# Five modulation units ahead of the S5 kernel rows, and two jobs handed to other engines, in a four-stage encoder trunk

## The chip, the cores and the metric

The kernel runs on one core of one Trainium2 chip. The core has five engines that run side by side and meet only at semaphores: TensorE (PE in the profile; PEld is its weight loading), VectorE (DVE), ScalarE (ACT), GpSimd (POOL) and SyncE (SP), which here only issues DMAs. The metric is the device time of one execution in microseconds (us); lower is better. Times inside an execution are counted from the start of the span that the profiler saw.

## The reference

One sequence of 512 tokens with 1024 features goes through an S5 layer and a differential-attention layer, each followed by a gated MLP with a causal convolution. Around each of the four stands a sandwich of norms and a modulation that comes from one conditioning vector:

```
for i in range(DEPTH):                       # DEPTH = 2
    mod = cond @ ada_w[i] + ada_b[i]         # 1024 x 6144, for one vector
    sh_t, sc_t, g_t, sh_c, sc_c, g_c = jnp.split(mod, 6, axis=-1)
    h = modulate(rms_norm(x, norm_g[i, 0]), sh_t, sc_t)
    h = s5_mixer(h, ...) if i % 2 == 0 else diff_attention(h, ...)
    x = x + g_t[:, None, :] * rms_norm(h, norm_g[i, 1])
    h = modulate(rms_norm(x, norm_g[i, 2]), sh_c, sc_c)
    h = conv_ffn(h, ffn_w_in[i], ffn_conv_w[i], ffn_conv_b[i], ffn_w_out[i])
    x = x + g_c[:, None, :] * rms_norm(h, norm_g[i, 3])
```

All is float32. The S5 mixer is a complex diagonal recurrence over the tokens for 64 groups of 16 channels, followed by a gelu and a gated product (GLU).

## The kernel before

**Precision and weights.** A large product is made of three matmuls: each operand is split into a rounded high part and the rest, its low part. Weights come in units of 128 x 2048 (1 MB) into two buffers `raw`. ScalarE copies a unit to `whi` (`split_high`, L803), and VectorE makes `wlo = raw - whi` (`split_low`, L1426; GpSimd does it for the first two units, L597). The semaphore `split_lo` counts the units whose low part is there.

**The first stage, S5.** In the first 126 us nothing is a plain product of that kind. In order of time:
- VectorE and GpSimd compute powers, input matrices and output matrices of the recurrence (`cl_re`, `cl_im`, `rot_c`, `rot_s`).
- TensorE turns the input matrices in four groups of four banks, `turned_inputs(0)` to `(3)` (L1952), and ScalarE copies each bank (`copy_inputs`, L747).
- Between them TensorE multiplies the conditioning vector with the 24 *modulation units* of layer 0, 1 MB each (`ada_unit`, L1913; unit n is `ada_raw` in the slot `ADA0_SLOT[n]`). Units 0 to 7 give the shift, 8 to 15 the second third of the row and 16 to 23 the last. All 24 add up in one PSUM bank, so the first unit of a third waits until ScalarE has copied the third before it out (`copy_row`, L727).
- The modulation of the first input is spread by one small matmul (L1977), and ScalarE applies it to the input u in 16 quarters (`scaled`, L759). The semaphore `u_ready` counts the four pieces of u.
- `inputs(piece)` (L1991) gives the driving term of the recurrence, which VectorE then scans (L1454 to L1482). `kernel_rows` (L2050) makes the 16 x 16 x 8 blocks of the short convolution, and after its last matmul ScalarE copies them (`kx`, L790), GpSimd adds the skip term (L583), and SyncE spreads them by 32 DMAs, eight to a piece, into four block-Toeplitz buffers `toep` that were cleared before (`load_toeplitz`, L333).
- `local(piece)` (L2009) multiplies u with a Toeplitz buffer, `carried(piece)` (L2027) adds what the state carries in, and `back(piece)` (L2038) turns the gelu of the sum, which is the operand of the GLU products (from L2129 on).

**Order.** Every engine runs a list written out by hand. SyncE's queue is one list as well: 24 modulation units, then the Toeplitz loads with the first two weight units between them. A load of a modulation unit waits until the unit that was in its slot before is used (`ada_used`). Slots 0 and 1 are the two `raw` buffers, slots 2 and 3 are the first two Toeplitz buffers, and slots 4 to 6 lie where the input matrices of `turned_inputs(2)` and `(3)` stood, so they are free only after these (`inb_psum`).

**Between the first MLP and attention** stands `barrier(1)`: sums of squares, two roots by GpSimd (L605), and then `next_input(1)` on VectorE, which per feature tile f gates the branch (`gate_late`, L1578), adds it to x (tiles 0 and 1 on VectorE, L1507, 2 to 7 on GpSimd, L608), scales it (`scale`, L1599) and makes the low part (`low`, L1586). TensorE follows tile by tile with the products for the attention values. After tile 3 VectorE also makes the low part of the value weights' second unit:

```
next_input(1, {3: lambda: split_low(U_V + 1, 1, None)})
```

Of the kernel before, what the change touches and what calls it, by code (L numbers as in the profile page):

```python
# [17 lines left out]
F32 = mybir.dt.float32  # L18
F32R = mybir.dt.float32r
I32 = mybir.dt.int32  # L20
ALU = mybir.AluOpType
# [3 lines left out]
P = 128  # L25
D = 1024
SEQ = 512
KT = D // P
# [11 lines left out]
OCTS = 4  # L40
# [21 lines left out]
ADA0_SLOT = 4 * (0, 1, 2, 3) + (6, 4, 5, 0, 1, 6, 4, 5)  # L62
# [14 lines left out]
def build(nc, a, out_rows):  # L77

    ctx = ExitStack()
    with ctx:  # L80
# [320 lines left out]
        def _(sp):  # L401
# [17 lines left out]
            for piece in range(OCTS):  # L419
                load_toeplitz(sp, piece)  # L420
                if piece % 2:
                    n = piece // 2
                    sp.wait_ge(ada_used, 20 + n)
                    sp.dma_start(raw[:, n, :], a["units"][n]).then_inc(raw_landed[n], 16)
# [60 lines left out]
        def _(pool):  # L485
# [73 lines left out]
            def decay_tile(piece):  # L559

                wait(pool, scanned, piece - 1)
                dst, g = decays[piece % 2], slice(PO * piece, PO * piece + PO)
                link(nc.gpsimd.tensor_copy(dst, s5s[:, 18, g].unsqueeze(2).broadcast_to([P, PO, NB])))
                nc.gpsimd.memset(dst[:, :, 0], 0.0).then_inc(decay_ready, 1)
# [7 lines left out]
            decay_tile(1)  # L572
# [6 lines left out]
            pool.wait_ge(ada_used, 2 * KT)  # L579
            for i in range(2):  # L580
                nc.gpsimd.memset(toep[i][:], 0.0).then_inc(toep_clear, 1)
            pool.wait_ge(k_copied, 4)
            nc.gpsimd.tensor_tensor(kx[:, 0], kx[:, 0], tk, ALU.add).then_inc(k_ready, 1)  # L583
            pool.wait_ge(hx_im, 2)
# [15 lines left out]
            def residual(r):  # L600

                pool.wait_ge(const_ready, 5)
                for root, ready, n in ((stat[:, 16:16 + QT], r1_ready, 1), (stat[:, 20:20 + QT], r2_ready, 2)):
                    pool.wait_ge(root_arg, 2 * r + n)
                    nc.gpsimd.tensor_tensor(root, nwt[:, 0, 0:QT], power[:], ALU.pow).then_inc(ready, 1)  # L605
                for f in POOL_X[r]:
                    pool.wait_ge(gated, KT * r + f + 1)
                    nc.gpsimd.tensor_tensor(x[:, f, :], x[:, f, :], y_of(r)[:, f, :], ALU.add).then_inc(x_pool, 1)  # L608
# [69 lines left out]
        def _(act):  # L678
# [101 lines left out]
            copy_inputs(3, partial(scaled, 0))  # L780
            for quarter in range(3):
                scaled(1, quarter)
            copy_row(1)
            store_row(1, 0)
            scaled(1, 3)
            for quarter in range(2):
                scaled(2, quarter)
# [5 lines left out]
            for quarter in range(2, 4):  # L793
                scaled(2, quarter)
            for quarter in range(4):
                scaled(3, quarter)
# [364 lines left out]
        def _(dve):  # L1161
# [574 lines left out]
            next_input(1, {3: lambda: split_low(U_V + 1, 1, None)})  # L1736
# [6 lines left out]

            split_low(U_V + 2, 0, None)
# [158 lines left out]
        def _(pe):  # L1903
# [54 lines left out]
            def ada_units(lo, hi):  # L1958

                for n in range(lo, hi):  # L1960
                    ada_unit(n)
# [13 lines left out]
            turned_inputs(2, (2, 3))  # L1975
            pe.wait_ge(umod_rhs, 2)
            M(psum[:, 7, P:P + 2 * GROUPS], sel16[:].rearrange("p t c -> p (t c)"),  # L1977
              ca[:, 0, 0:2 * GROUPS], start=True, stop=True).then_inc(umod_psum, 1)
            turned_inputs(3)
            ada_units(13, 14)  # L1980
# [77 lines left out]
            ada_units(14, 15)  # L2058
# [4 lines left out]
            ada_units(15, 16)  # L2063
            kernel_rows(range(2, 4))
            ada_units(16, 17)
            kernel_rows(range(4, 6))
            ada_units(17, 18)
            kernel_rows(range(6, PO)).then_inc(k_psum, 1)
            inputs(1)
            ada_units(18, 20)  # L2070
            carried(0, True)
            ada_units(20, 22)
            inputs(2)
            ada_units(22, N_ADA_PE)
            local(0, False)
            carried(1, True)
            inputs(3)
            local(1, False)
# [571 lines left out]
```

## Time and profile before

| | |
|---|---|
| Median of 3 runs | 1212.21 us (1211.85 to 1215.84) |
| The profiled execution: its own time, its span | 1210.92 us, 1209.1 us |
| PE busy | 1171.6 us, 97% of the span |
| DVE, ACT, POOL busy | 61%, 43%, 33% |
| The chain that ended last | PE 83%, DVE 9%, issue 2%, SP queue 2%, ACT 2% |
| Busy in 100 to 110 us | PE 9.88, DVE 8.13, ACT 7.01, POOL 1.49 of 10 us |

The profile comes from one execution. TensorE is busy nearly all the time, so what counts is where it is idle or slow, and that is the first 126 us and the barriers. The chain that ended last is followed back from the last instruction, at each step to what released it; a part of it on another engine than TensorE is a place where the kernel waited for that engine. [...]

### The profile page before, as it was taken

The page shows a single profiled execution, that of the slowest core. Times are in us where ns is not written, and L with a number is a line of the kernel's source. Part 1 is how long each engine was busy: PE and PEld are TensorE (multiplying, and loading weights), DVE is VectorE, ACT ScalarE, POOL GpSimd, SP SyncE. Part 2 cuts the span into 40 slices and gives each one's busy share as a digit, 9 for nine tenths or more (in the row PEclk, how much of TensorE's full clock was granted, in tenths as well). Part 3 has the DMA queues.
Part 4 walks back from the last instruction along what each step waited for, and adds up shares of the span by engine and source line. Part 5 has one row for each costly group of instructions (what it writes and reads, how often), then busy time and mean ns, then how long its engine had stood idle before and what let it go on. Part 6 is the DMA issues. An engine that isn't in the chain of part 4 may idle for free.

```text
span 1209.1 us, 17510 instructions
## 1 busy us (share of the span) xinstructions
PE 1171.6 (97%) x6508; PEld 934.6 (77%) x6508; DVE 737.0 (61%) x974; ACT 520.0 (43%) x792; POOL 393.8 (33%) x272
## 2 busy tenths in 40 slices
PE   5789999999999999999999999999999999999998
PEld 2458888788787888888787777677788888888887
DVE  8998687979863553243854777948644444442323
ACT  4466444443443342143423677755434443442311
POOL 4973100366553431000305345402343334420000
PEclk9999999999999999999999999999999999999999
DMA  9887655177633323231223322211222222223221
GB/s 374 339 271 179 260 204 207 45 268 255 249 122 105 104 75 135 103 106 70 83 105 105 105 78 80 88 35 70 105 105 76 97 104 104 91 97 125 92 82 70
DMA packets 34984, 162.25 MB, mean 134 GB/s; under 512 B 12768, under 2 KB 13088, under 8 KB 16688
## 3 DMA queue, kind: packets, MB, share of 16 engines
q1 hardware_dynamic: 25632, 161.15, 37.5%
q10 hardware_dynamic: 9296, 0.34, 0.6%
q8 instruction: 37, 0.61, 0.2%
q14 instruction: 19, 0.16, 0.0%
HBM read 152.79 MB, written 2.13 MB: 128 GB/s over the span
## 4 chain that ended last, share of the span: by engine, by line
PE 83%; DVE 9%; issue 2%; SPq 2%; ACT 2%; POOL 1%; DMA 1%; DVEq 0%; POOLq 0%; ACTq 0%
PE psum L2095 17%; PE psum L2097 17%; PE psum L2096 17%; PE psum L2361 3%; PE psum L2360 3%; PE psum L2362 3%; PE psum L2263 3%; PE psum L2264 3%; PE psum L2265 3%; SPq L333 2%; PE psum L2421 1%; PE psum L2442 1%; PE psum L2409 1%; PE psum L2129 1%; PE psum L2403 1%
## 5 line engine op out<-in xcount | busy, mean ns | idle before, releaser
L2095 PE MATMUL psum<-hhi,whi 128*128 128x512 f32 x896 | 352.0, 393 | 0.9 <-DVE wlo L1426 0.9
L2097 PE MATMUL psum<-hhi,wlo 128*128 128x512 f32 x896 | 348.9, 389 | 0.0
L2096 PE MATMUL psum<-hlo,whi 128*128 128x512 f32 x896 | 348.8, 389 | 0.0
L1426 DVE TENSOR_TENSOR wlo<-raw,whi 128x2048 fp32r<-128x2048 f32 x79 | 187.9, 2378 | 185.0 <-ACT whi L803 185.0
L803 ACT ACTIVATE whi<-raw 128x2048 fp32r<-128x2048 f32 x80 | 153.2, 1914 | 166.9 <-PE psum L2362 74.3
L615 POOL TENSOR_TENSOR ca<-ca,cb 128x512 f32<-128x512 f32 x44 | 137.6, 3126 | 235.7 <-ACT ca L963 235.7
L2095 PEld LDWEIGHTS psum<-hhi,whi 128*128 128x128 f32 x896 | 168.5, 188 | 38.5 <-issue 2.1
L2097 PEld LDWEIGHTS psum<-hhi,wlo 128*128 128x128 f32 x896 | 168.2, 188 | 35.1
L2096 PEld LDWEIGHTS psum<-hlo,whi 128*128 128x128 f32 x896 | 168.3, 188 | 34.1
L1626 DVE SCALAR_TENSOR_TENSOR ca<-psum,convp,ca 128x511 f32<-128x511 f32 x44 | 32.9, 749 | 182.6 <-ACT ca L958 182.6
L965 ACT ACTIVATE ghi<-ca 128x512 f32 (+1 forms) x44 | 27.8, 633 | 149.4 <-POOL ca L615 149.4
L958 ACT ACTIVATE ca<-psum,convp 128x512 f32<-128x512 f32 x44 | 34.2, 778 | 114.2 <-PE psum L2097 106.7
L617 POOL TENSOR_TENSOR glo<-ca,ghi 128x512 f32 (+1 forms) x44 | 67.8, 1542 | 40.3 <-ACT ghi L965 40.3
L605 POOL TENSOR_TENSOR stat<-nwt,power 128x4 f32<-128x4 f32 x6 | 6.4, 1069 | 220.2 <-DVE nwt L1555 216.3
L2263 PE MATMUL psum<-whi,ghi 128*128 128x512 f32 x176 | 68.7, 391 | 0.0
L2265 PE MATMUL psum<-whi,glo 128*128 128x512 f32 x176 | 68.5, 389 | 0.0
L2264 PE MATMUL psum<-wlo,ghi 128*128 128x512 f32 x176 | 68.5, 389 | 0.0
L2360 PE MATMUL psum<-ghi,whi 128*128 128x512 f32 x176 | 68.5, 389 | 0.0
L2361 PE MATMUL psum<-glo,whi 128*128 128x512 f32 x176 | 68.5, 389 | 0.0
L2362 PE MATMUL psum<-ghi,wlo 128*128 128x512 f32 x176 | 68.5, 389 | 0.0
L1493 DVE SCALAR_TENSOR_TENSOR ada_acc<-ada_ring,cond,ada_acc 128x2048 f32<-128x2048 f32 x24 | 62.4, 2602 | 0.0
L1055 ACT ACTIVATE prob<-psum,stat 128x128 f32<-128x128 f32 (+3 forms) x64 | 33.1, 523 | 17.7 <-DVE stat L1772 17.3
(411 smaller groups left out, 1846.5 us busy)
## 6 DMA issues: line engine op xcount, KB each, us to landing
raw<-in_units SPq DMA_DIRECT2D x92, 1024.0 KB, 4.8
ada_raw<-in_ada_w SPq DMA_DIRECT2D x24, 1024.0 KB, 8.2
ada_ring<-in_ada_w SPq DMA_DIRECT2D x24, 1024.0 KB, 4.8
qk_sw<-ca SPq DMA_DIRECT2D x32, 128.0 KB, 2.3
u<-in_x_blocks SPq DMA_DIRECT2D x1, 2048.0 KB, 9.7
x<-in_x_t SPq DMA_DIRECT2D x1, 2048.0 KB, 8.2
out_rows<-y_late SPq DMA_DIRECT2D x8, 256.0 KB, 2.0
bc_par<-in_s_bc SPq DMA_DIRECT2D x1, 1024.0 KB, 4.9
```

Source lines behind the costliest of these rows:

```text
L615: nc.gpsimd.tensor_tensor(ca[:, s, :], ca[:, s, :], cb[:, s, :], ALU.mult).then_inc(g_ready, 1)
L803: A(whi[:, s, :], raw[:, s, :], ACT.Copy).then_inc(split_hi, 1)
L1426: TT(wlo[:, s, :], raw[:, s, :], whi[:, s, :].bitcast(F32), ALU.subtract).then_inc(split_lo, 1)
L2095: M(out, w_hi, hi[:, k, :], start=(k == 0), stop=False)
L2096: M(out, w_hi, lo[:, k, :], start=False, stop=False)
L2097: return M(out, w_lo, hi[:, k, :], start=False, stop=(k == KT - 1))
L2263: M(out, ghi[:, row, tok], whi[:, s, w], start=(isinstance(v, int) and row == 0), stop=False)
L2264: M(out, ghi[:, row, tok], wlo[:, s, w], start=False, stop=False)
L2265: return M(out, glo[:, row, tok], whi[:, s, w], start=False, stop=(isinstance(v, int) and row == JT - 1))
L2360: M(out, whi[:, s, w], ghi[:, row, :], start=(fixed and row == 0), stop=False)
L2361: M(out, whi[:, s, w], glo[:, row, :], start=False, stop=False)
L2362: return M(out, wlo[:, s, w], ghi[:, row, :], start=False, stop=(fixed and row == JT - 1))
```

## The change

Five things change:
- **TensorE's order.** Units 13 to 17 now come before `inputs(0)`; before, units 14 to 17 stood after it. Two units stay between the kernel rows (18 and 19, where three stood), and units 20 to 23 follow `inputs(1)` in one piece. `local(1)` moves ahead of `inputs(3)`.
- **Slots.** Units 17 to 23 get other slots, so that units 17 and 18 need no slot of the input matrices.
- **ScalarE.** The copy of the second third of the modulation row (`copy_row(1)`) moves between the scaling of quarters 2 and 3 of the first piece, its store right after that, and all of piece 1 is scaled ahead of the wait for the kernel rows. ScalarE clears the first Toeplitz buffer (128 x 2048), with a copy of a zero column.
- **GpSimd** clears only the second Toeplitz buffer, and does it after it has added the skip term.
- **The value weights' second unit.** Its low part is made by GpSimd in `barrier(1)`, after the two roots and ahead of the six additions to x; VectorE no longer makes it.

```
-ADA0_SLOT = 4 * (0, 1, 2, 3) + (6, 4, 5, 0, 1, 6, 4, 5)
+ADA0_SLOT = 4 * (0, 1, 2, 3) + (6, 0, 1, 4, 5, 0, 1, 6)
...
             decay_tile(0)
-            decay_tile(1)
...
-            pool.wait_ge(ada_used, 2 * KT)
-            for i in range(2):
-                nc.gpsimd.memset(toep[i][:], 0.0).then_inc(toep_clear, 1)
             pool.wait_ge(k_copied, 4)
             nc.gpsimd.tensor_tensor(kx[:, 0], kx[:, 0], tk, ALU.add).then_inc(k_ready, 1)
+            decay_tile(1)
+            pool.wait_ge(toep_clear, 1)
+            pool.wait_ge(ada_used, 2 * KT)
+            nc.gpsimd.memset(toep[1][:], 0.0).then_inc(toep_clear, 1)
...
+                if r == 1:
+                    pool.wait_ge(split_hi, U_V + 2)
+                    nc.gpsimd.tensor_tensor(wlo[:, 1, :], raw[:, 1, :], whi[:, 1, :].bitcast(F32),
+                                            ALU.subtract).then_inc(split_lo, 1)
...
-            copy_inputs(3, partial(scaled, 0))
-            for quarter in range(3):
+            def scaled_first(quarter):
+
+                scaled(0, quarter)
+                if quarter == 2:
+                    copy_row(1)
+
+            copy_inputs(3, scaled_first)
+            store_row(1, 0)
+            for quarter in range(4):
                 scaled(1, quarter)
-            copy_row(1)
-            store_row(1, 0)
-            scaled(1, 3)
-            for quarter in range(2):
-                scaled(2, quarter)
+            act.wait_ge(const_ready, 5)
+            act.wait_ge(ada_used, 2 * KT)
+            A(toep[0][:].rearrange("p k q c -> p (k q c)"), ac_w[:, W_A, 1:2].broadcast_to([P, UNIT]),
+              ACT.Copy).then_inc(toep_clear, 1)
             act.wait_ge(k_psum, 1)
...
-            next_input(1, {3: lambda: split_low(U_V + 1, 1, None)})
+            next_input(1, {})
...
+            dve.wait_ge(split_lo, U_V + 2)
             split_low(U_V + 2, 0, None)
...
             turned_inputs(2, (2, 3))
+            ada_units(13, 15)
             pe.wait_ge(umod_rhs, 2)
...
-            turned_inputs(3)
-            ada_units(13, 14)
+            turned_inputs(3, (0, 1))
+            ada_units(15, 16)
+            turned_inputs(3, (2, 3))
+            ada_units(16, 18)
...
             inputs(0)
-            ada_units(14, 15)
...
             kernel_rows(range(0, 2))
-            ada_units(15, 16)
-            kernel_rows(range(2, 4))
-            ada_units(16, 17)
-            kernel_rows(range(4, 6))
-            ada_units(17, 18)
-            kernel_rows(range(6, PO)).then_inc(k_psum, 1)
+            ada_units(18, 19)
+            kernel_rows(range(2, 5))
+            ada_units(19, 20)
+            kernel_rows(range(5, PO)).then_inc(k_psum, 1)
             inputs(1)
-            ada_units(18, 20)
+            ada_units(20, N_ADA_PE)
             carried(0, True)
-            ada_units(20, 22)
             inputs(2)
-            ada_units(22, N_ADA_PE)
             local(0, False)
             carried(1, True)
+            local(1, False)
             inputs(3)
-            local(1, False)
             back(0)
```

TensorE's list from `turned_inputs(2, (2, 3))` to the first kernel rows, before (L1952 `turned_inputs`, L1977 the small matmul of the modulation, L1913 a modulation unit, L1991 `inputs`, L2050 the kernel rows; `ada_raw_79` to `_85` are slots 0 to 6):

```order
L1952 MATMUL psum<-ident,lb_69 128x128 x16
L1977 MATMUL psum<-ca,sel_96 128x128
L1952 MATMUL psum<-ident,lb_70 128x128 x32
L1913 MATMUL psum<-ada_raw_80,cond 1x512 x4
L1991 MATMUL psum<-u,inb_re 64x64 x16
L1991 MATMUL psum<-u,inb_im 64x64 x16
L1913 MATMUL psum<-ada_raw_81,cond 1x512 x4
L2050 MATMUL psum<-cl_re,kb 16x128 x8
```

The same stretch of the changed kernel (its line numbers are 10 to 13 higher):

```order
L1962 MATMUL psum<-ident,lb_69 128x128 x16
L1923 MATMUL psum<-ada_raw_80,cond 1x512 x4
L1923 MATMUL psum<-ada_raw_81,cond 1x512 x4
L1988 MATMUL psum<-ca,sel_96 128x128
L1962 MATMUL psum<-ident,lb_70 128x128 x16
L1923 MATMUL psum<-ada_raw_82,cond 1x512 x4
L1962 MATMUL psum<-ident,lb_70 128x128 x16
L1923 MATMUL psum<-ada_raw_85,cond 1x512 x4
L1923 MATMUL psum<-ada_raw_79,cond 1x512 x4
L2004 MATMUL psum<-u,inb_re 64x64 x16
L2004 MATMUL psum<-u,inb_im 64x64 x16
L2063 MATMUL psum<-cl_re,kb 16x128 x8
```

Units 13 and 14 now stand ahead of the small matmul, unit 15 inside `turned_inputs(3)`, and 16 and 17 between it and `inputs(0)`; behind `inputs(0)` the kernel rows follow at once.

GpSimd's list around the skip term, the lines that go (-) and come (+); `toep_75` and `toep_76` are the first two Toeplitz buffers:

```order
 L563 COPY decay<-s5s 128x512
 L564 MEMSET decay 128x8
+L576 TENSOR_TENSOR cb<-sel_96,dskip 128x256
+L579 TENSOR_TENSOR kx<-kx,cb 128x256
 L563 COPY cb<-s5s 128x512
 L564 MEMSET cb 128x8
-L577 TENSOR_TENSOR cb<-sel_96,dskip 128x256
-L581 MEMSET toep_75 128x2048
-L581 MEMSET toep_76 128x2048
-L583 TENSOR_TENSOR kx<-kx,cb 128x256
+L583 MEMSET toep_76 128x2048
```

The addition to `kx` has moved ahead of the second decay tile and of the one clearing that is left here.

GpSimd's list of the changed kernel in `barrier(1)`, from the two roots on:

```order
L605 TENSOR_TENSOR stat<-nwt,power 128x4 x2
L608 TENSOR_TENSOR wlo<-raw,whi 128x2048
L612 TENSOR_TENSOR x<-x,y_late 128x512 x6
L635 TENSOR_TENSOR gdiag<-ident,gate 128x1024
L645 TENSOR_TENSOR qk<-ca,cosb 128x512 x2
```

The row L608 is new: before, the six additions followed the roots directly.

## Rows read from the trace of the kernel before

**Rows 1.** Chain of waits, 53 to 111 us: start, us, what.

```profile
53.10 1.63 PE psum L1952 x8
...
65.16 1.75 PE psum L1913 x8
...
67.98 0.97 PE psum L1913 x8
...
75.00 2.07 ACT kx L790 x4
...
78.43 0.60 SPq L333
...
103.33 4.37 DMA toep<-kx
...
110.74 3.66 PE psum L2027 x128
```

**Rows 2.** Timeline of PE: start, us, what, xcount [idle before <-releaser].

```profile
52.62 0.49 PE L1977 MATMUL psum<-ca,sel 128*128 128x128 f32 x2 [2.51 <-DVE ca L1399]
...
62.30 1.16 PE L1991 MATMUL psum<-u,inb_re 128*64 128x64 f32 x32 [2.97 <-ACT u L759]
...
74.87 1.15 PE L1991 MATMUL psum<-u,inb_re 128*64 128x64 f32 x32
...
76.88 1.90 PE L1913 MATMUL psum<-ada_raw,cond 128*1 128x512 f32 x16
...
106.53 1.10 PE L2038 MATMUL psum<-ident,z 128*128 128x128 f32 x8
```

**Rows 3.** Windows: length, busy PE PEld DVE ACT POOL, PEclk, DMA, GB/s.

```profile
54.00:55.00 1.00, 1.00 (x7) 1.00 (x6) 0.96 (x3) 0.19 (x1) 0.84 (x3) 0.50 0.89 369
...
64.00:65.00 1.00, 1.00 (x22) 0.97 (x19) 0.69 (x3) 1.00 (x4) 0.85 (x1) 0.50 1.03 434
```

**Rows 4.** Timeline of ACT, 60 to 106 us.

```profile
60.72 5.41 ACT L759 ACTIVATE u<-u,s5s 128x64 f32<-128x64 f32 x16
69.01 0.60 ACT L727 ACTIVATE sq<-psum 128x512 f32<-128x512 f32 x1 [2.88 <-PE psum L1913]
69.64 1.05 ACTq L732 DMA_DIRECT2D mod_rows<-sq  x1
...
103.99 1.93 ACT L803 ACTIVATE whi<-raw 128x2048 fp32r<-128x2048 f32 x1
```

**Rows 5.** DMA view, issued 42.40 to 42.67 us (unit 14): KB, us to landing.

```profile
ada_raw<-in_ada_w SPq DMA_DIRECT2D x1, 1024.0 KB, 9.6
```

**Rows 6.** DMA view, issued 60.00 to 60.40 us (unit 20).

```profile
ada_raw<-in_ada_w SPq DMA_DIRECT2D x1, 1024.0 KB, 12.1
```

**Rows 7.** Timeline of DVE, the scans of the recurrence.

```profile
81.59 1.39 DVE L1460 TENSOR_TENSOR v_re<-v_re,ca 128x512 f32<-128x512 f32 x1
...
107.69 0.69 DVE L1482 SCALAR_TENSOR_TENSOR rot_c<-v_re,rot_s 128x504 f32<-128x504 f32 x1
```

**Rows 8.** Timelines of POOL, DVE and PE in barrier(1), and POOL at 108 us.

```profile
581.09 1.01 POOL L605 TENSOR_TENSOR stat<-nwt,power 128x4 f32<-128x4 f32 x1 [1.34 <-DVE nwt L1573]
586.17 2.55 POOL L608 TENSOR_TENSOR x<-x,y_late 128x512 f32<-128x512 f32 x2 [4.06 <-DVE y_late L1578]
...
584.02 0.69 DVE L1507 TENSOR_TENSOR x<-x,y_late 128x512 f32<-128x512 f32 x1
...
588.76 0.74 DVE L1586 SCALAR_TENSOR_TENSOR hlo<-psum,modt,hhi 128x512 fp32r<-128x512 f32 x1
...
591.53 2.94 DVE L1426 TENSOR_TENSOR wlo<-raw,whi 128x2048 fp32r<-128x2048 f32 x1
...
589.65 1.10 PE L2409 MATMUL psum<-whi,hlo 128*128 128x512 f32 x4
...
596.44 1.20 PE L2409 MATMUL psum<-whi,hlo 128*128 128x512 f32 x4 [1.15 <-DVE hlo L1586]
...
108.51 4.62 POOL L597 TENSOR_TENSOR wlo<-raw,whi 128x2048 fp32r<-128x2048 f32 x1 [14.05 <-DVE rot_c L1482]
```

More of the change, by code:

```diff
@@ L422, in _ @@
                     n = piece // 2
-                    sp.wait_ge(ada_used, 20 + n)
+                    sp.wait_ge(ada_used, 22 + n)
                     sp.dma_start(raw[:, n, :], a["units"][n]).then_inc(raw_landed[n], 16)
@@ L792, in _ @@
                   ACT.Copy).then_inc(k_copied, 1)
[L793 to L796, printed above, removed]
+            for piece in range(2, OCTS):
+                for quarter in range(4):
+                    scaled(piece, quarter)
             def split_high(n, s, half):
```

## The prediction

> **What bounds the kernel now.** I read the busy times first: TensorE works 97% of the span, so a change pays only where TensorE is idle or slow and everything behind it hangs on that place. Then the chain of waits, in order of time, for the stage that the diff touches. It runs over the last group of turned matrices and ScalarE's scaling to `inputs(0)` at 62.30, over a modulation unit (65.16) to the kernel rows, and at 75.00 it leaves TensorE for ScalarE's copy of them [rows 1, 2]. GpSimd's addition follows, and from 78.43 on the chain is SyncE's queue: 32 Toeplitz loads one after another until the last one, issued at 103.33, lands at 103.33 + 4.37 = 107.70 [rows 1]. Only then can `local(3)` run, then `back(2)` and `carried(3)`, which ends at 110.74 + 3.66 = 114.40 [rows 1], and the GLU products start.
>
> [...] First, TensorE's own list is as long as the queue: its last work ahead of `local(3)`, a `back`, ends at 106.53 + 1.10 = 107.63 [rows 2], 0.07 us before the load lands. So both must get shorter together. [...]
>
> VectorE is the third list. It computes without a pause and ends its part of the stage at 107.69 + 0.69 = 108.38 [rows 7]; the last quarter of `carried(3)`, which needs that result, begins about 0.9 us before 114.40, so there are 5 us of room.
>
> The other place is `barrier(1)`. VectorE's `wlo` (2.94 us from 591.53) holds back the low part of tile 3, and TensorE idles 1.15 us for it at 596.44 [rows 8].
>
> **The kernel rows, part by part.**
>
> *Unit 14 ahead of the small matmul.* Its load is issued at about 42.5 and takes 9.6 us [rows 5], so it is there at 52.1. One unit takes 0.97 us [rows 1] and the small matmul starts at 53.1 where it started at 52.62 [rows 2]: 0.5 late. Unit 13 fills the gap before that and costs nothing.
>
> *The first eight transposes behind it.* They took 1.63 us at half clock [rows 1]; eight of the same shape take 1.10 at full clock (the `back`) [rows 2]. With two units in the 2.51 us gap I expect the full clock: 0.5 early.
>
> *ScalarE's copy of the modulation row* is now inside the chain: 0.60 [rows 4], of which 0.1 overlaps its neighbour: 0.5 late. The three together put `inputs(0)` at 62.30 + 0.5 - 0.5 + 0.5 = 62.8.
>
> *Units 15, 16 and 17.* TensorE has to wait in `turned_inputs(3)` for ScalarE's copies anyway, so unit 15 is free. Unit 16 begins a new third and waits for `copy_row(1)`, which ScalarE reaches about 2.4 us before its last scaling ends: one copy and one quarter (5.41 / 4 = 1.35 us [rows 4]) stand behind it. Units 16 and 17 need 2 x 0.97 = 1.94 us, so they end just before 62.8. They are hidden by the same scaling that TensorE idled for; without that cover they would cost 1.94.
>
> *`inputs(0)` and unit 14.* At half clock they took 65.16 - 62.30 = 2.86 and 1.76 (to 66.92, as 65.16 + 1.75 says) [rows 1, 2]. At full clock `inputs` takes 76.88 - 74.87 = 2.01 [rows 2], and unit 14 is gone. I take the full clock: 62.8 + 2.01 = 64.8.
>
> *The kernel rows.* From 66.92 to 75.00 there are 8.08 us with three units; two units stay, so 8.08 - 0.97 = 7.11. They end at 64.8 + 7.1 = 71.9 instead of 75.0. **That is 3.1 us.** Of it, 1.76 + 0.97 are two units that left the stretch, 0.85 is the clock, and 0.5 is given back in front.
>
> *What could hold ScalarE up.* After the first piece, at 62.7, it issues the store (1.05), scales piece 1 (16 instructions, 5.41) and clears a Toeplitz buffer, an operation that no row shows. Its nearest row is the copy of a 128 x 2048 unit, 1.93 [rows 4]; a bound below is nothing, one above is GpSimd's 4.62 for that size [rows 8]. With 1.93 ScalarE is at the kernel rows at 62.7 + 1.1 + 5.4 + 1.9 = 71.1, 0.8 us ahead of 71.9. At 4.62 it would be 1.9 us late, and the gain 1.2.
>
> *The loads.* SyncE is past its last modulation unit before the rows end, and the loads of 17 and 18 go out at 50 to 51 us, in a stretch where the queue waited for a slot. GpSimd reaches `kx` early, for it clears nothing before. So the first Toeplitz load goes out at 78.43 - 3.1 = 75.3, and the last lands at 104.6. Everything that GpSimd does later (second decay tile, second clearing) is needed 6 us after that at the earliest.
>
> *TensorE's list from there.* It has 2 units fewer behind the rows (6 before, 4 now: 1.9 us) and starts 3.1 us earlier, but `carried(1)` and `carried(2)` wait for VectorE, whose times stay. Counting the list through with the full-clock durations it is at `local(3)` at 104 to 105, level with the load at 104.6. `local(1)` ahead of `inputs(3)` swaps two waits that are both over by then. So the GLU products start 3.1 us earlier. If the Toeplitz loads got through faster, because units 22 and 23 no longer share the DMA engines with them, VectorE's waits would cap it at about 3.7.
>
> **`barrier(1)`.** The wait of 1.15 goes. GpSimd's second root ends at 581.09 + 1.01 = 582.10; its `wlo` takes 4.62 [rows 8] and ends at 586.7. The addition for tile 2 began at 586.17, so it is 0.55 late. VectorE's scaling of tile 2 and the low part of tile 1 queue behind it. That low part ended at 588.76 + 0.74 = 589.50 and TensorE took it at 589.65 [rows 8], so 0.4 of it reach TensorE. VectorE's own addition at 584.02 has two SBUF operands and runs beside the new instruction; such an instruction took 1.39 instead of 0.69 beside GpSimd [rows 7, 8], so up to 0.7. The two overlap in the same queue: I take 0.65, between 0.4 and 1.1. Net 1.15 - 0.65 = **0.5 us**, between 0 and 0.75.
>
> **Sum.** 3.1 + 0.5 = 3.6 us from the profiled execution's own 1210.9, so 1207.3. The median of the runs lies 1.3 above that execution, and I predict on it: 1212.2 - 3.6 = 1208.6.
>
> **The rivals.**
>
> *A, the clock falls all the same.* TensorE is through `turned_inputs(3)` at about 58.2 and idles until `copy_row(1)` is done at 60.4: a gap of 2.2 us, hardly shorter than the two that were followed by half clock [rows 2, 3]. For it: those two. Against it: it has units on both sides. If units 16, 17 and `inputs(0)` run at half clock, that costs what it cost before, about 0.85 + 0.8 = 1.7 us: 1210.3. [...]
>
> *B, VectorE or the DMA engines become the bound.* GpSimd's additions fall on other VectorE instructions than before. Three prolonged as in [rows 7], by 0.7 each, would delay VectorE by 2.1 and `carried(1)` and `carried(2)` with it: the gain falls to about 1.5, 1210.7. For it: VectorE has no idle time there to make it up. Against it: GpSimd has less to do than before in that stretch.
>
> *C, slower: a load is late.* Unit 17 is now needed at 61.6, about 11 us after its load can be issued; before, it had 14. All of `inputs(0)` stands behind it. At 12.1 us, the longest of this stretch [rows 6], it comes at 62.7 and costs 1.1. It decides from 14.6 us on, when the 3.6 are used up; at 19 us the time would be 1216.6. Against it: only unit 16's load and older ones stand ahead of it.
>
> *D, VectorE is shut out in `barrier(1)`.* If its addition at 584.02 has to wait until GpSimd's `wlo` ends at 586.7, it is 2.65 late, and so is TensorE: 1.15 - 2.65 = -1.5, with the 3.1 a gain of 1.6: 1210.6. Against it: an instruction of that kind was 0.70 longer beside GpSimd, not shut out [rows 7]. [...]
>
> *E, more.* The full cap (3.7) and a barrier with little loss (0.75 to 1.15): 1207.5.
>
> **How the numbers follow.** Forecast 0.44 (1207.9 to 1209.4, since each term moves by some tenths), A 0.22, B 0.12, C 0.06, D 0.05, E 0.11. A range of 1207.1 to 1211.0 leaves out C, a part of E and the far ends of A, B and D, about 0.2. About 0.3% (3.6 us) is what a measurement of this kernel can tell from no change, and the forecast lies on that bound. Faster by more: half of the forecast's cases (0.22), all of E, and 0.07 of A and B where their price is half of the one above: 0.40. Within: 0.54. Slower: 0.06.
>
> **What would show it.** Right: the copy of `kx` starts near 71.9, the first Toeplitz load near 75.3, the last lands near 104.6, `carried(3)` ends near 111.3; the clock is 1.00 from 53 to 67; TensorE has no idle ahead of L1977 but 1 us before unit 14, and one of about 2 us before unit 16; in `barrier(1)` the idle ahead of the low step of tile 3 is gone and 0.6 stands ahead of that of tile 0 or 1. Wrong: a clock of 0.50 anywhere between 59 and 67 (A); VectorE's last scan after 109 (B); TensorE's idle time ahead of unit 14, 17 or 18 put down to a DMA (C); ScalarE's clearing above 2.7 us; or a stall behind 126 us that takes back what the first stage gave.

## The result

The change makes the kernel slower, by half a per cent.

| | before | after |
|---|---|---|
| Median of 9 runs each, same chip | 1211.85 us (1209.68 to 1215.84) | 1218.49 us (1216.14 to 1221.55) |
| Ratio, 95% interval | | 1.0052 [1.0041, 1.0063] |
| The profiled execution: own time, span | 1210.92, 1209.1 us | 1219.39, 1217.6 us |

Forecast was 1208.6 (1207.1 to 1211.0), with 0.06 for slower: wrong in sign. The medians differ by 6.6 us and the two profiled executions by 8.5: that of before lies 0.9 below its median, that of after 0.9 above its own. The 8.5 us between the two spans can be followed by anchors: the first GLU product starts 4.5 later (118.83 instead of 114.32), `barrier(1)` adds 2.9, and the attention stage some 1.0, where TensorE waits 3.0 us in all for `att` (L1797) instead of 2.0. That last 1.0 I did not follow further.

**Up to the kernel rows the profile after is what the forecast drew.** Timeline of PE, columns as in [rows 2]:

```profile
52.23 1.04 PE L1923 MATMUL psum<-ada_raw,cond 128*1 128x512 f32 x8 [1.04 <-DMA ada_raw<-in_ada_w]
...
60.81 1.90 PE L1923 MATMUL psum<-ada_raw,cond 128*1 128x512 f32 x16 [2.52 <-ACT sq L731]
62.64 1.15 PE L2004 MATMUL psum<-u,inb_re 128*64 128x64 f32 x32
```

Units 16 and 17 hide in the wait for ScalarE, `inputs(0)` starts at 62.64 (62.8 forecast) and the first row at 64.66 (64.8). Then comes what no step of the forecast had:

```profile
69.28 0.31 PE L2063 MATMUL psum<-cl_re,kb 64*16 64x128 f32 x5 [1.76 <-issue]
...
76.85 0.39 PE L2063 MATMUL psum<-cl_im,kb 64*16 64x128 f32 x1 [4.49 <-issue]
...
78.24 1.97 PE L2004 MATMUL psum<-u,inb_re 128*64 128x64 f32 x32
...
81.85 4.18 PE L1923 MATMUL psum<-ada_raw,cond 128*1 128x512 f32 x32
```

In the middle of the rows TensorE stands still twice, for 1.76 and 4.49 us, and the profile names no releaser: "issue" is time in which it waited for nothing that the profile shows. `inputs(1)` behind it takes 3.61 us (78.24 to 81.85) instead of the 2.01 of [rows 2]. ScalarE then waits for TensorE (timeline of ACT):

```profile
67.68 1.91 ACT L796 ACTIVATE toep<-ac_w 128x2048 f32<-128x2048 f32 x1
78.35 2.06 ACT L800 ACTIVATE kx<-psum 128x512 f32<-128x512 f32 x4 [8.76 <-PE psum L2063]
```

ScalarE's clearing took 1.91 (1.93 forecast), and then it idled 8.76 us for the rows. Windows of the stretch show the clock (PEclk, the granted share of full speed; 0.50, which in before stands behind the idle times of 2.51 and 2.97 us [rows 2, 3], is "half clock" below) and the DMA engines (columns as in [rows 3]), first after, then before:

```profile
70.00:73.00 3.00, 2.37 (x94) 1.01 (x79) 2.96 (x5) 0.00 (x0) 2.52 (x4) 1.00 0.96 391
73.00:75.00 2.00, 0.00 (x0) 0.00 (x0) 1.97 (x3) 0.00 (x0) 0.00 (x0) 1.00 0.46 188
75.00:77.00 2.00, 0.15 (x8) 0.15 (x16) 1.90 (x4) 0.00 (x0) 0.00 (x0) 0.80 0.05 12
77.00:80.00 3.00, 3.00 (x66) 2.48 (x56) 1.08 (x2) 1.65 (x4) 0.00 (x0) 0.50 0.02 5
```

```profile
70.00:73.00 3.00, 2.40 (x77) 1.15 (x81) 2.96 (x5) 2.26 (x7) 2.81 (x7) 1.00 0.15 33
```

After has the DMA engines full until 73.5 us; before had them nearly idle (0.15) in 70 to 73. VectorE runs out of work in 77 to 80 as well (busy 1.08 of 3 us). And the DMA view has, beside the kernel's own queue, one called "instruction", with packets of 16 KB (37 packets, 0.61 MB on the page of after and on that of before). These are the windows 74.6 to 74.7 us of after and 71.8 to 71.9 us of before (queue, kind: packets, MB, share):

```profile
q8 instruction: 1, 0.02, 58.2%
```

```profile
q8 instruction: 1, 0.02, 59.9%
```

Before has a packet at 71.83 and after none until 74.63, 1.1 us after the engines drained, and TensorE resumes 2.2 us behind it.

**In `barrier(1)`**, timelines of POOL, DVE and PE after, answering to [rows 8]:

```profile
586.62 4.81 POOL L608 TENSOR_TENSOR wlo<-raw,whi 128x2048 fp32r<-128x2048 f32 x1
...
588.56 3.42 DVE L1516 TENSOR_TENSOR x<-x,y_late 128x512 f32<-128x512 f32 x1
...
594.08 1.28 PE L2417 MATMUL psum<-whi,hlo 128*128 128x512 f32 x4 [2.48 <-DVE hlo L1595]
595.15 0.63 PE L2411 MATMUL psum<-whi,hhi 128*128 128x512 f32 x1
```

VectorE's addition takes 3.42 us instead of 0.69. It ends at 591.98, 0.55 us after GpSimd's subtraction (586.62 + 4.81 = 591.43). TensorE idles 2.48 for it, and its next matmuls start 0.43 apart instead of 0.23: half clock (0.50 from 596 to 598). Against the first product of the stage (589.52, before 584.98) the low step of tile 5 stands 2.9 us later than before (609.44, before 602.01).

### The profile page after: what moved, and what is told of

Same layout as the page of the kernel before. It is cut to its first block, busy times and chain, and to the rows that moved or that the text cites. A ratio compares the mean times of both kernels' runs of the same rounds, so it can differ in the third digit from the quotient of the medians.

```text
span 1217.6 us, 17514 instructions
## 1 busy us (share of the span) xinstructions
PE 1173.3 (96%) x6508; PEld 935.7 (77%) x6508; DVE 739.1 (61%) x973; ACT 521.5 (43%) x793; POOL 397.2 (33%) x272
## 4 chain that ended last, share of the span: by engine, by line
PE 85%; DVE 5%; DMA 3%; issue 2%; SPq 2%; ACT 1%; POOL 1%; DVEq 0%; POOLq 0%; ACTq 0%
PE psum L2103 17%; PE psum L2105 17%; PE psum L2104 17%; PE psum L2368 3%; PE psum L2370 3%; PE psum L2369 3%; PE psum L2273 3%; PE psum L2271 3%; PE psum L2272 3%; SPq L333 2%; PE psum L2429 1%; DMA ada_raw<-in_ada_w 1%; PE psum L2417 1%; PE psum L2411 1%; PE psum L2412 1%
```

## The experiments

Two theories stood against each other for the rows. **F**: TensorE's instructions come through the same DMA engines, and their packet waits behind the modulation loads in the queues. **L**: the new order itself, five rows on end without a unit, uses instructions up faster than they come. For the barrier: **P**, VectorE's addition is shut out while GpSimd works, against **Q**, something else. "Rows" below is the start of ScalarE's copy of `kx`, "GLU" the first product of L2129; before has 75.00 and 114.32. A ratio is to the kernel before, run on the same chip beside the experiment, with its 95% interval in brackets. Experiments 4 to 7 were timed once: they are read by their traces, not by their times.

**1. The barrier's part alone.** To the kernel before, only this is added, with its wait on VectorE:

```
+                if r == 1:
+                    pool.wait_ge(split_hi, U_V + 2)
+                    nc.gpsimd.tensor_tensor(wlo[:, 1, :], raw[:, 1, :], whi[:, 1, :].bitcast(F32),
+                                            ALU.subtract).then_inc(split_lo, 1)
-            next_input(1, {3: lambda: split_low(U_V + 1, 1, None)})
+            next_input(1, {})
+            dve.wait_ge(split_lo, U_V + 2)
```

> The kernel before, with one part of the change: the low part of the value weights' second unit made by GpSimd. The rest is as before. Theory P (VectorE's addition of tile 1 is shut out for as long as GpSimd's instruction runs, TensorE idles 2.5 us for it and falls to the half clock): the addition takes about 3.4 us instead of 0.69, TensorE idles about 2.5 us ahead of the first low step and runs the next 3 us at half clock, the time rises by 3 to 4.5 us. Rival Q (what the profile of the changed kernel shows in the barrier is a consequence of the disturbed first stage, and by itself the step is worth the 0.5 us of the prediction): 0 to 1 us faster.

Ratio 1.0019 [1.0008, 1.0030], span 1210.3. Timelines of DVE and PE:

```profile
583.31 3.42 DVE L1511 TENSOR_TENSOR x<-x,y_late 128x512 f32<-128x512 f32 x1
```

```profile
588.83 1.20 PE L2414 MATMUL psum<-whi,hlo 128*128 128x512 f32 x4 [2.48 <-DVE hlo L1590]
```

The same 3.42 and 2.48, so P. The clock stayed at 1.00 behind it in this execution, and the stage cost 1.3 us, not 2.9: the 1.6 between them is the half clock that the execution of after had behind the same gap (eight matmuls 0.43 apart instead of 0.23). The 3 to 4.5 us that I had expected for the whole were too many: the ratio makes 2.3.

**2. The first stage's part alone:** the changed kernel with `barrier(1)` as before.

```
-                if r == 1:
-                    pool.wait_ge(split_hi, U_V + 2)
-                    nc.gpsimd.tensor_tensor(wlo[:, 1, :], raw[:, 1, :], whi[:, 1, :].bitcast(F32),
-                                            ALU.subtract).then_inc(split_lo, 1)
-            next_input(1, {})
+            next_input(1, {3: lambda: split_low(U_V + 1, 1, None)})
-            dve.wait_ge(split_lo, U_V + 2)
```

> The changed kernel with the value weights as before, so the first stage's part of the change alone. Both theories of the first stage expect two idle stretches of TensorE inside the kernel rows, about 1.8 and 4.5 us, put down to nothing that the profile shows, and 2 to 4.5 us more than the kernel before. Rival Q expects most of the change's 6.6 us here, 6 us or more.

Ratio 1.0021 [1.0009, 1.0032], span 1213.6. Issue stalls of 1.15 and 2.84 us in the rows, rows 78.17, GLU 118.14. The stalls are shorter than in after, in the same places. Each part costs some 2.4 us by itself; the product of the two ratios, 1.0040, is near the whole's 1.0052 and leaves 1.4 us that lie within the intervals.

**3. Units 22 and 23 loaded late.** As 2, but their loads wait for the end of the rows:

```
+                if n == N_ADA_PE - 2:
+                    sp.wait_ge(k_psum, 1)
                 sp.dma_start(ada0_raw[slot][:], ...)
```

> As e2_s5_only, but SyncE waits until the kernel rows are done before it issues the loads of modulation units 22 and 23. Theory F (TensorE's next instructions are fetched by the same DMA engines and come behind the modulation loads that are queued there): the DMA engines run dry near 70 us, the long idle stretch of 4.5 us in the kernel rows shrinks to under 1 us, the rows end at 72 to 74 instead of 78, and units 22 and 23 are waited for instead, 1 to 3 us; the time is 2 to 5 us below e2_s5_only, and at or below the kernel before. Theory L (the list itself is the cause: with fewer long matmuls between the small ones TensorE uses up its instructions faster than they can come, whatever the DMA engines do): the idle stretches stay, and the time is that of e2_s5_only or above it, for the late loads cost extra.

Ratio 1.0005 [0.9993, 1.0017]. Stalls 1.82 and 0.65, rows 75.42, GLU 116.30. TensorE's list is that of 2, and of the long stall 0.65 is left: F. The late units are waited for, 1.49 and 2.05 us, a little more than the 1 to 3 that I had expected, and the copy starts at 75.42, not at 72 to 74, for the first stall stayed. The intervals of 2 and 3 overlap, so it is the trace that shows the gain, not the time.

**4. Units 21 to 23 loaded in part.** As 2, with 128 of 2048 columns of these units loaded, so that part of layer 0's modulation comes from old data:

```
+                c = slice(0, UNIT if n < N_ADA_PE - 3 else P)
+                sp.dma_start(ada0_raw[slot][:, c], a["ada_w"][n][:, c])...
```

> As e2_s5_only, but the loads of modulation units 21 to 23 bring the first 128 of 2048 columns only, so part of the modulation of layer 0 is made of old data; everything else is computed. Theory F: the DMA engines are idle from about 68 us, the long idle stretch in the kernel rows goes (under 0.7 us), and the rows end near 72 to 73. Theory L: it stays at 4 us or more, since TensorE's list is the same.

1213.01 us (one run), stalls 1.84 and 0.37, rows 74.28. Same list, no long stall, no late unit. The first stall stayed, and with it the rows are later than the 72 to 73 that I had expected.

**5. Also units 17 and 18 in part.** As 4, with `n in (17, 18, 21, 22, 23)` cut.

> This is the changed kernel with barrier(1) as in the kernel before, and the loads of units 17, 18 and 21 to 23 bring only the first 128 of 2048 columns (part of layer 0's modulation is then made from old data); units 16, 19 and 20 are loaded whole. TensorE's list is unchanged. The question is the first of the two stalls in the kernel rows, the one near 70 us that the profile puts down to issue (1.15 us in the run with units 21 to 23 whole, 1.84 with them small). Theory F (TensorE's instructions are fetched through the same DMA engines, and the fetch waits behind the modulation loads in the queue): with some 2 MB less in the queue between 58 and 70 us the packet of instructions that starts at 67.6 to 68.5 in the runs so far starts 1.5 to 5 us earlier, and the first stall shrinks below 0.5 us; no second stall; the rows end at 72.0 to 72.8, kx at 72 to 73. Rival L (the rows' small matmuls use up the instructions faster than any fetch brings them): the stall stays at 1.1 to 1.9 us wherever the packet starts.

1209.49 us (one run), span 1207.7. The packets of instructions come at 65.46 and 69.46, and timeline of PE:

```profile
71.86 0.28 PE L2059 MATMUL psum<-cl_im,kb 64*16 64x128 f32 x1 [0.50 <-issue]
```

Both stalls together are 0.50, rows 72.73, GLU 111.70. A second profile of this kernel (14) has 0.59. So the first stall too was the queue's.

**6. The kernel before with more traffic.** TensorE's list untouched; two copies of 1 MB from DRAM to DRAM ahead of the load of unit 21, which nothing reads:

```
+                if n == N_ADA_PE - 3:
+                    for i in range(2):
+                        sp.dma_start(spare[i], a["units"][i]).then_inc(par_in, 16)
```

> This is the kernel before, TensorE's list unchanged, with two copies of 1 MB from DRAM to DRAM that nothing reads, which SyncE issues behind the load of unit 20 (about 60 us), so that the DMA engines stay busy from 69.75 to 73.25 us, where they were idle in the kernel before (share 0.08 and less) and where its packet of instructions at 71.83 came. Theory F: that packet comes when the copies have drained, at 74 to 76 us, and the kernel rows get a stall of 2 to 4 us put down to issue that the kernel before does not have (its only one there is 0.61 us); the rows end at 77 to 79 instead of 74.9, and the span grows by 2 to 4 us. Rival L (the stall comes from TensorE's own order, five rows in a row without a unit): no stall over 1 us in the rows, since the order is that of before, and the rows end by 75.5; the loads of units 21 to 23 may land up to 5 us later in either case, which the waits for them would show as DMA.

1217.53 us (one run), span 1215.7. Timeline of PE, and windows:

```profile
77.76 0.37 PE L2054 MATMUL psum<-cl_re,kb 64*16 64x128 f32 x1 [3.02 <-issue]
```

```profile
70.00:72.00 2.00, 1.45 (x32) 0.38 (x33) 1.97 (x4) 1.16 (x4) 1.88 (x5) 1.00 0.96 414
...
78.00:80.00 2.00, 2.00 (x42) 1.52 (x28) 0.40 (x1) 1.20 (x3) 0.00 (x0) 0.50 0.95 389
```

The packet of 71.83 comes at 75.33, and the order of before gets the stall and the half clock of after. This is the reverse of 3 to 5: traffic alone makes the stall, whatever the order. L falls. No unit was waited for. The span grew by 6.6 us where I had expected 2 to 4; the copy of the rows starts 3.8 later than in before and the GLU 5.8 (120.08).

**7. GpSimd's `wlo` behind VectorE's additions.** As 1, with a wait ahead of it:

```
+                    pool.wait_ge(x_dve, 2 * KT - len(POOL_X[0]) - len(POOL_X[1]))
```

> This is the kernel before with GpSimd making the low part of the value weights' second unit, as in the first experiment, but only after VectorE's second addition to x (GpSimd waits for it). Theory P (the two exclude each other: an addition with both operands in SBUF stands still while GpSimd works): VectorE's addition takes 0.69 us again instead of 3.42, GpSimd's low part runs from 584.7 to 589.5 us and the additions of tiles 2 to 7, now GpSimd's next work, start at 589.5 instead of 586.2; TensorE waits 1.5 to 2.5 us for the high or low part of tile 2 and hardly after that. Rival Q' (the 3.42 us came from a slow access to these addresses, whatever GpSimd does): the addition still takes 3 us or more.

1220.34 us (one run). Timelines of DVE and PE:

```profile
588.31 0.69 DVE L1512 TENSOR_TENSOR x<-x,y_late 128x512 f32<-128x512 f32 x1
```

```profile
597.02 2.07 PE L2415 MATMUL psum<-whi,hlo 128*128 128x512 f32 x4 [2.92 <-DVE hlo L1591]
```

The addition takes 0.69 again, beside an idle GpSimd: P holds, Q' falls. My 1.5 to 2.5 us for TensorE was low: it waits 2.92, and with the half clock behind it (0.50 from 597 to 601) the stage is 4.5 us longer than before. 4.3 of the span's growth lay ahead of the barrier, with the first stage as before but an issue stall of 2.02 and a Toeplitz wait of 3.32 us: one execution of the old order differs from another by so much.

**8. Units 22 and 23 behind `inputs(2)`**, and else as 3:

```
-            ada_units(20, N_ADA_PE)
+            ada_units(20, 22)
             carried(0, True)
             inputs(2)
+            ada_units(22, N_ADA_PE)
```

> This is the changed kernel with barrier(1) as before, the load of unit 22 (and 23 behind it) held until the kernel rows are done, and, new in this run, units 22 and 23 moved behind inputs(2), where the kernel before had its last two. Theory F: the long stall stays gone as in the run with the late loads (0.65 us left there), and the two waits for the late loads (1.49 and 2.05 us there, with a stretch at half clock behind them) shrink below 0.5 us together, since the units come some 6 us later; the first stall of 1 to 2 us stays. Carried(0) ends near 82; the ratio to the kernel before is 0.997 to 1.000. Rival M (the waits move on to the next late thing, the Toeplitz pieces, which the loads of units 22 and 23 at 76 to 81 us delay): the waits for Toeplitz data before local(1) to local(3) add up to over 2 us and the ratio stays at 1.000 to 1.001.

Ratio 1.0005 [0.9984, 1.0027]. The waits for units are gone, as expected, but a new issue stall of 1.95 stands in `inputs(2)` at 84.76, where the Toeplitz loads, which stand behind the held loads in the queue, fill the engines (DMA share 1.13 in 82 to 84 us), and `local(3)` waits 2.25 for its piece. GLU 116.28, as in 3. This is rival M.

**9. The low part one tile later**, in the kernel before: `next_input(1, {4: ...})`.

> This is the kernel before with one number changed: VectorE makes the low part of the value weights' second unit after tile 4 of next_input(1) instead of after tile 3. Theory W (the wait of 1.15 us at 596.4 is only the low part of tile 4 behind 2.94 us of VectorE, and one tile later TensorE is further behind): the wait before the low-part matmuls of tile 4 goes, VectorE starts the weight's low part near 594, and at most 0.5 us is given back at tile 5; 0.5 to 1.2 us gained, a ratio of 0.9990 to 0.9997. Rival (the lead is no larger one tile on, since VectorE needs 2.12 us per tile and TensorE 2.75): a wait of 0.9 to 1.5 us at tile 5 takes its place, and the ratio is 1.000 within 0.0005.

Ratio 0.9999 [0.9985, 1.0012]. The wait of 1.15 is gone and 0.40 stands at the next tile; from the first product to the low step of tile 5 the stage is 0.6 us shorter. That is W's size in the trace, and the interval neither shows it nor rules it out.

**10, 11 and 12. The loads held back further.** 10 is the kernel before with `if n == 19: sp.wait_ge(k_psum, 1)`; 11 adds the edit of 9; 12 is 8 with `n == 20` and the edit of 9.

> This is the kernel before, TensorE's list unchanged, with the load of unit 19 (and those of 20 to 23 behind it) held until the kernel rows are done. Theory F (instructions are fetched behind the queued loads): only three loads (16 to 18) are in the queue from 58 us, the DMA engines are free from about 67 to 74.5 us, the packets of instructions near 68 and 72 us find them idle and start 0.5 to 2 us earlier, and the stall put down to issue in the rows (0.61 us in one execution of before, 1.06 and 2.02 us in two others with the same order) is below 0.5 us. The five loads then come from 74.5 to 87 us: unit 19 is waited for up to 0.7 us at 77.8 us, and the Toeplitz pieces, 32 DMAs behind them, may land up to 2 us later. Net a ratio of 0.9985 to 1.0005. Theory L (the rows outrun any fetch): the stall keeps its 0.6 to 2.0 us and the late loads only add, a ratio of 1.0005 to 1.003.

> This is the kernel before with both edits: the loads from unit 19 on held until the kernel rows are done, and the low part of the value weights' second unit after tile 4. The two places are 500 us apart, so the gains should add: a ratio of 0.9980 to 1.0000 if theories F and W hold, 0.9995 to 1.0030 if neither does.

> This is the changed kernel with barrier(1) as before but the low part after tile 4, units 22 and 23 behind inputs(2), and the loads from unit 20 on held until the kernel rows are done. Four loads (16 to 19) are in the queue from 58 us and drain by 67.5 us. Theory F: the stall put down to issue near 70 us (1.52 us with five loads in the queue) falls to 0.5 us or less, the rows end at 72.5 to 73.5 us, unit 20 is waited for 0 to 1.5 us, and VectorE, which works without a pause from 68.9 us on, is the next limit, as the reading of before had it as a rival. Ratio 0.9980 to 0.9995. Rival M (the loads held back come into the way of the Toeplitz pieces and of the packets of instructions near 82 us, where the run before this had a stall of 1.95 us): the gain in the rows is given back by 112 us, ratio 0.9995 to 1.0010.

| | ratio | issue stalls in the rows | rows | waits for units | GLU |
|---|---|---|---|---|---|
| 10 | 1.0053 [1.0034, 1.0072] | none | 72.76 | 2.08, 2.50 | 119.17 |
| 11 | 1.0048 [1.0033, 1.0063] | none | 74.71 | 4.44, 0.33 | 122.79 |
| 12 | 1.0011 [0.9996, 1.0027] | none | 72.93 | 2.88, 1.41 | 116.75 |

In all three the stall in the rows is gone, with either order, which is F once more. And in all three the time is lost again, against the ratios that I had expected (0.9985 to 1.0005, 0.9980 to 1.0000 and 0.9980 to 0.9995): the first held unit (19, in 12 unit 20) comes 2.1 to 4.4 us late, not the 0.7 that I had, since its load started only at the end of the rows and took 4.9, 7.3 and 4.8 us to land in 10, 11 and 12. Holding loads back made no room here; in 10 it costs as much as the whole change.

**13 and 14. Both orders without the load pressure.** Five units loaded in part in each, with the modulation partly from old data: 13 is the kernel before with units 19 to 23 cut, 14 is the kernel of 5, timed.

> This is the kernel before, TensorE's list unchanged, in which the loads of units 19 to 23 bring only the first 128 of 2048 columns (part of layer 0's modulation is then made from old data): the control of the next run. With the DMA engines free from about 67 us on, theory F expects no stall over 0.5 us put down to issue in the rows, kx at 74.0 to 74.9, and, the Toeplitz pieces being alone in the queue, the first GLU product at 112.5 to 114; a ratio of 0.997 to 0.9995 to the kernel before. If the forecast's 3.1 us of order were real, this run must be slower than the next one.

> This is the changed kernel with barrier(1) as before, in which the loads of units 17, 18 and 21 to 23 bring only their first 128 columns, as in a run before, now timed beside its control. In both runs five loads are cut and the DMA engines are free from about 67 us, so the difference between the two is TensorE's order (and ScalarE's and GpSimd's part) without the loads. Theory O (the forecast's reading of the order was right: the rows end 3.1 us earlier once nothing holds the instructions up, and what follows keeps it): kx at 72 to 73, the first GLU product 1.5 to 3 us before that of the control, and a ratio lower by 0.0012 to 0.0025 than the control's. Rival B (VectorE and the Toeplitz pieces are the bound behind the rows): kx is earlier by 2 us or more, but the first GLU product by less than 0.8 us, and the ratios agree within 0.0007.

| | ratio | stall in the rows | rows | GLU | span |
|---|---|---|---|---|---|
| 13, old order | 0.9995 [0.9981, 1.0010] | 0.28 | 73.81 | 113.73 | 1210.1 |
| 14, new order | 0.9986 [0.9975, 0.9997] | 0.59 | 72.73 | 110.95 | 1207.0 |

In these two profiles the new order starts the rows' copy 1.1 us and the GLU 2.8 us earlier; by the medians it is 1213.11 against 1211.55, 1.6 us, and the intervals overlap. The ratio is lower by 0.0009, less than Theory O asked for and more than rival B did. A gain of the order, where the loads are taken away, is likely by this and not shown: there is one profile of the control, and the old order by itself has its GLU anywhere between 113.62 and 118.64. With all loads in place no version with the new order is faster than the kernel before (after, 2, 3, 8 and 12 have ratios of 1.0005 to 1.0052).

## Why the prediction was wrong

- **Unit 14, the transposes, `copy_row(1)`: right.** `inputs(0)` at 62.64 instead of 62.8.
- **Units 15 to 17 hidden, full clock in `inputs(0)`: right in this execution (2.02 us), by luck.** Of the eight profiles with the new order six have the half clock here (rival A): units 16 and 17 take 2.34 to 3.58 us instead of 1.90 in 2, 3, 5, 8, 12 and 14, and in 2, 3 and 14 `inputs(0)` is partly slow too. Of the eight with the old order five have it in 61 to 67 us and three (7, 10 and 13) do not. So the 0.85 us that the sum booked as the clock's share of the 3.1 was the state of one execution, not something the old order costs and the new one gives back.
- **"The kernel rows. 8.08 - 0.97 = 7.11. They end at 71.9": this is the step that failed.** It took the rows' length as fixed. From 64.7 they took 13.6 us: 7.1, plus 6.25 of stall less the 0.61 that the 7.11 already held, plus some 0.9 at half clock for the rest of them. Experiments 3, 4, 5, 8, 12 and 14 bring the long stall down to 0.65 us or less with the new order, 6 puts one into the old order.
- **"The loads."** I asked of each load whether its data would be in time, and they were. But units used earlier also free their slots earlier and so pull the loads forward: unit 21 is issued at 62.8 us instead of 71.9, and 22 and 23 at 66.8 and 67.2 instead of 73.9 and 78.0. In before the engines were nearly idle from 69.75 to 73.25 us because SyncE was waiting for a slot, and it was in that gap that a packet of instructions came. I had counted only what the data's users wait for. Order and slots changed together and were not tried apart, so which of them pulled the loads forward by how much is open. What TensorE waited behind such a packet of 16 KB came to 4.49 us in one place, and the forecast had no term for it.
- **What the stall costs behind it.** The rows are 3.35 us later than before and the GLU 4.5: the first Toeplitz load goes out at 81.32 instead of 78.43, and the last lands at 112.2 instead of 107.7. That the end of the rows carries over to the GLU one to one held only roughly: 39.3 us between the two before, 40.5 after, 39.0 in 5, but 43.2 and 42.6 in the executions of 9 and 7, which have the old order here and in which TensorE waited 3.73 and 3.32 us for the last Toeplitz load. How much of the 4.5 in after the stall alone made is therefore not known; experiment 2 prices the stage as a whole, at 2.5 us.
- **ScalarE's clearing (1.93): right**, 1.91.
- **Rivals.** A was not in this execution but in six of the other seven with this order. B and C did not happen: VectorE ended its part at 112.31 (111.63 + 0.68), past the 109 that was B's sign, but it had run out of work before, while TensorE stood still and then ran at half clock. C came nearest in sign with the wrong mechanism, a load late for its user.
- **"`barrier(1)`. VectorE's own addition has two SBUF operands and runs beside the new instruction; up to 0.7": wrong, and rival D right.** The wait of 1.15 went as said. The addition was 2.73 us longer, and experiment 7 gives the 0.69 back by keeping GpSimd out of its way. The error was the row that I measured by. I read the 1.39 of [rows 7], 81.59 to 82.98, as a price of 0.7 for any meeting. GpSimd's timeline of before has beside it:

```profile
81.38 1.05 POOL L547 TENSOR_TENSOR ssum<-rot_s,rot_c 128x496 f32<-128x496 f32 x1
82.51 1.48 POOL L548 TENSOR_TENSOR rot_s<-rot_s,ssum 128x496 f32<-128x496 f32 x1
```

  The first ends at 82.43 and VectorE's instruction 0.55 us later; the second ends at 83.99 and VectorE's next one (82.90 to 84.54) again 0.55 later, as in the barrier of after (0.55) and of experiment 1 (0.54). So the trace of before already showed a block until GpSimd is done, on a short instruction; here GpSimd's lasts 4.81 us. That was a row for D, which I had given 0.05 with none named for it, and both profiles that have the pair of the barrier show it (3.42 us). The engines do not meet only at semaphores, as I had put it at the outset: VectorE had started its addition and was held up in it, with no wait ahead of it. D's price of -1.5 was near the -1.3 of experiment 1; the half clock behind the gap made it 2.9 in the profiled execution of after.

No version here beats the kernel before: 9 is equal to it, and 14 leaves loads out. Open is why the last 1.0 us of the profiled execution is lost in attention. That the packets on the instruction queue are TensorE's is inferred from when they come: of the 32 stalls put down to issue that the profiles of the sixteen kernels have between 62 and 112 us, 31 end 2.2 to 2.9 us after the start of such a packet, and one 3.35.

## What to carry to other kernels

Here, where TensorE runs hundreds of small matmuls, packets of instructions came through the DMA engines too, and late where loads filled these (share 0.96; a packet 2.8 us later in after than in before, 3.5 in experiment 6), with stalls of 4.49 and 3.02 us: look at the instruction queue in the DMA view before you close a gap in the loads. A stall put down to issue amid full DMA engines is first to be held against the packets, before it is called a property of the list: 31 of 32 ended 2.2 to 2.9 us behind the start of one here. Before a clock in one profile is booked as a gain, a second execution of the same kernel should be looked at: with the same order around it `inputs(0)` had 1.00 or 0.50 here. And a GpSimd instruction with SBUF operands is to be held against what VectorE has to do with two SBUF operands while it lasts (3.42 us instead of 0.69 beside one of 4.81 here), and against the clock that TensorE may lose when it then waits (0.50 behind 2.48 us in after, 1.00 in experiment 1).

## What the hardware showed that I had not expected

- A packet of 16 KB on the instruction queue took 0.9 to 1.5 us once it ran, in the sixteen profiles between 60 and 112 us (1.9 in one case of experiment 11), but one came 3.5 us later behind 2 MB of other traffic (71.83 to 75.33, experiment 6).
- A VectorE addition of two 128 x 512 SBUF operands took 3.42 us beside a GpSimd subtraction of 128 x 2048 in two executions, and 0.69 with GpSimd idle. In four pairs VectorE's instruction with two SBUF operands ended 0.54 to 0.55 us after the GpSimd instruction beside it. With a PSUM operand two others kept 0.68 and 0.76 us beside the subtraction (after, at 586.90 and 587.90).
- TensorE's clock was 0.50 from about 76.2 to 83 us; it fell within the last microsecond of the stall of 4.49 us (0.93 in 76.00 to 76.25, 0.50 in 76.25 to 76.50). It fell also in `barrier(1)` behind an idle time of 2.48 us in after (0.50) but not in experiment 1 (1.00), with the same idle time.
- The first stage of the kernel before, unchanged, had stalls put down to issue of 0.61, 1.06, 0.49 and 2.02 us in the rows in four executions, and the first GLU product from 113.62 to 118.64.
